# A hybrid decoder layer on one core: twenty of the merge gates by a seven-product scheme in a stage of their own, merge and output in one stage

## What is computed

```python
xn = rmsnorm(x, norm_pre)
z = jnp.einsum('bld,dn->bln', xn, w_in)
aq, ak, av, ag, bq, bfg, bi, bg, cu, cg, mg = split_in(z)
...
gates = jax.nn.sigmoid(mg.reshape(b, L, N_BRANCH, D_MODEL))
merged = (gates[:, :, 0] * (y_a @ w_br_a) + gates[:, :, 1] * (y_b @ w_br_b)
          + gates[:, :, 2] * (y_c @ w_br_c))
out = merged @ w_out
return x + rmsnorm(out, norm_post), new_kv, s_new.astype(dt), pool_new
```

## Time and profile before

| what | us |
|---|---|
| median of three runs | 1928.43 |
| profiled execution, its own time | 1930.2 |
| its span | 1928.4 |
| PE busy (share of the span) | 1886.4 (98%) |
| DVE, POOL, ACT busy | 726.8, 460.1, 355.9 |
| DMA | 159.25 MB, mean 83 GB/s |

### The profile page before, as it was taken

How to read it: one execution, slowest core, us unless ns; L and a number is a source line. 1 busy time by engine, 2 the same in 40 slices (tenths; PEclk the granted TensorE clock), 3 DMA queues, 4 the chain that set the end, 5 groups by cost and what they waited for, 6 DMA issues and landing times. The chain is left out here.

```text
span 1928.4 us, 34551 instructions
## 1 busy us (share of the span) xinstructions
PE 1886.4 (98%) x13648; PEld 1814.0 (94%) x13648; DVE 726.8 (38%) x1271; ACT 355.9 (18%) x876; POOL 460.1 (24%) x266
## 2 busy tenths in 40 slices
PE   7999999999999999999999999999999999999898
PEld 6999998999999999999999999998999999999897
DVE  6223123123222316655755664657200132211523
ACT  5121121122022110111011011122111221111321
POOL 2321222122122121222212222132333333333300
PEclk9999999999999999999999999999999999999999
DMA  5424315322432330221121122123422232212522
GB/s 157 112 68 93 111 53 109 89 74 48 127 92 63 76 94 23 68 67 39 50 67 45 55 66 61 32 79 144 134 68 67 79 103 84 84 56 84 206 89 88
DMA packets 240804, 159.25 MB, mean 83 GB/s; under 512 B 35277, under 2 KB 226125, under 8 KB 240716
## 3 DMA queue, kind: packets, MB, share of 16 engines
q1 hardware_dynamic: 202844, 124.16, 22.7%
q10 hardware_dynamic: 37872, 33.79, 5.3%
HBM read 123.48 MB, written 34.44 MB: 82 GB/s over the span
## 5 line engine op out<-in xcount | busy, mean ns | idle before, releaser
L232 PE MATMUL psum<-x_hi,w_hi 128*128 128x384 f32 (+1 forms) x2496 | 820.8, 334 | 9.6 <-PEq L129 2.8
L232 PE MATMUL psum<-x_lo,w_hi 128*128 128x384 f32 (+1 forms) x2496 | 804.3, 327 | 0.0
L232 PEld LDWEIGHTS psum<-x_hi,w_hi 128*128 128x128 f32 x2496 | 469.9, 188 | 23.5 <-issue 13.8
L232 PEld LDWEIGHTS psum<-x_lo,w_hi 128*128 128x128 f32 x2496 | 470.3, 188 | 0.0
L232 PE MATMUL psum<-x_hi,w_lo 128*128 128x384 f32 (+1 forms) x2496 | 461.3, 326 | 0.0
L206 POOL CAST w_hi<-w_raw 128x1024 fp32r<-128x1024 f32 (+1 forms) x128 | 136.7, 1068 | 1343.7 <-PE psum L232 1063.2
L232 PEld LDWEIGHTS psum<-x_hi,w_lo 128*128 128x128 f32 x2496 | 418.0, 188 | 0.0
L208 POOL TENSOR_TENSOR w_lo<-w_raw,w_hi 128x1024 fp32r<-128x1024 f32 (+1 forms) x128 | 310.4, 2425 | 10.2
L2023 ACT ACTIVATE a_feature<-psum 128x384 f32<-128x384 f32 (+1 forms) x100 | 45.2, 452 | 355.1 <-PE psum L232 355.1
L2135 DVE TENSOR_TENSOR a_prob<-psum,band 128x128 f32<-128x128 f32 (+1 forms) x64 | 21.5, 378 | 204.8 <-PE psum L1829 203.6
L232 PE MATMUL psum<-mb_y_hi,w_hi 128*128 128x384 f32 (+1 forms) x192 | 62.2, 329 | 2.4 <-DVE mb_y_lo L695 2.4
(11 more groups left out here) (249 smaller groups left out, 2074.0 us busy)
## 6 DMA issues: line engine op xcount, KB each, us to landing
w_raw<-in_w_in SPq DMA_DIRECT2D x104, 512.0 KB, 3.9
s_cached<-in_cache_kv_w SPq DMA_DIRECT2D x128, 64.0 KB, 2.6
s_cached<-in_cache_kv_w SPq DMA_DIRECT2D x64, 128.0 KB, 2.4
merged_rows<-c_ext ACTq DMA_DIRECT2D x15, 544.0 KB, 3.1
a_feature<-group_weights SPq DMA_DIRECT2D x12, 512.0 KB, 6.2
spare<-branch_outputs SPq DMA_DIRECT2D x10, 544.0 KB, 5.4
branch_outputs<-b_gate ACTq DMA_DIRECT2D x8, 544.0 KB, 3.1
c_ext<-merged_rows SPq DMA_DIRECT2D x8, 544.0 KB, 3.8
```

The lines of the kernel that those rows point to most:

```text
L232: mm = pe.matmul(psum[:, c, 0:n], w[:, s, k, :], x[:, k, t0:t0 + n], start=step is first, stop=step is last)
```

## The change

**A stage for gates.** `gate_phase` stands between `norm_phase` and `attention_phase`. The norm stage now begins with two gate tiles of branch B (instead of the first two attention tiles), and twenty more gates, B4 to B7, A0 to A7 and C0 to C7, are computed as ten pairs. A pair is a 1024 x 256 block of weights: its two tiles and the two halves of K make four blocks, and the two halves of K and of the tokens cut the activations into four quarters. Seven products of a block with a quarter (K 512, 544 tokens) take the place of eight. For that, four sums of quarters are formed once, by DVE and POOL, as `g_tmp`, and split into `g_sum_hi` (ACT) and `g_sum_lo` (DVE, and one by POOL); four sums of weight blocks are formed for each pair by DVE (`w_sums`); POOL splits the seven blocks, ACT and DVE combine the results, ACT applies the sigmoid, and the gates go to DRAM (`gates_d`). A product is two halves of 272 tokens with 12 matmuls each. PE's part is written out, not looped. The stage ends with the first attention tile (`project(pe, SLOTS, 0, ...)`), and a second `fresh_semaphores` follows.

**One stage for merge and output.** `final_phase` takes the place of the two merge stages. The two gates B0 and B1 stay where they were. PE multiplies the eight B tiles one after the other, then A and C tiles in turn, with no gate between; the gates come from DRAM. The A and C outputs are split into `x_hi` and `x_lo`, which the normalized input no longer needs, during the B tiles. A merged tile is split at once into `y_hi` and `y_lo`, and is not stored and loaded again. Half of the first output weights are loaded and split during the A and C tiles. The output itself is as before.

The core of the diff (the lines of the two old stages are left out; of `gate_phase` parts of POOL, PE, ACT and DVE follow in this order, of `final_phase` parts of PE, ACT and DVE):

```diff
-            norm_phase(first_of((COL_AQ, COL_AK)), q0)
+            norm_phase(first_of((COL_MG + D + 2 * P, COL_MG + D + 3 * P)), q0)
+            gate_phase(first_of((COL_AQ, COL_AK)), q0)
+            fresh_semaphores()
             attention_phase(first_of((COL_BF, COL_BQ)), q0)
...
-            merge_phase("mb", 0, merge_b, True, bufs, (gate, graw), 3,
-                        ([*spare, so_far], [y_d[Y_A + k] for k in range(4)]), first_of((COL_MG, COL_MG + 2 * D)))
-            merge_output_phase("mac", Y_A, merge_ac, bufs, (gate, graw), 4, [col(w_out, 0), col(w_out, P)])
+            final_phase(bufs, (gate, graw))
...
+        def gate_phase(then, q0):
+            PAIRS = 10
+            HK, HN, N = KO // 2, NT // 2, NT // 4
+            RING = 4
...
+                    def split(n, r):
+                        m = 7 * n + r
+                        if r in (0, 3, 6):
+                            pool.wait_ge(raw_in[n % 2], 32 * (n // 2 + 1))
+                        else:
+                            pool.wait_ge(s_ready, 4 * n + {1: 1, 2: 2, 4: 3, 5: 4}[r])
+                        if m < RING:
+                            cv.projected(pool, 1 - m // 2, NCH - 1)
+                        else:
+                            pool.wait_ge(done, 2 * (m - RING) + 2)
+                        pool.tensor_copy(ring(w_hi, m), source(n, r)).then_inc(p_hi_ready, 1)
+                        pool.wait_ge(p_hi_ready, m + 1)
+                        pool.tensor_tensor(ring(w_lo, m), source(n, r), ring(w_hi, m).bitcast(F32), ALU.subtract)\
+                            .then_inc(p_ready, 1)
+                    pool.tensor_tensor(tmp[1][:, :, :], quarter(x_hi, 0, 0).bitcast(F32),
+                                       quarter(x_lo, 0, 0).bitcast(F32), ALU.add).then_inc(x11_ready, 1)
+                    pool.wait_ge(t_full, 3)
+                    pool.tensor_tensor(tmp[0][:, :, :], tmp[2][:, :, :], tmp[0][:, :, :], ALU.subtract)\
+                        .then_inc(t3_full, 1)
+                    for r in range(2):
+                        split(0, r)
+                    pool.wait_ge(t_hi_ready, 3)
+                    pool.wait_ge(t3_full, 1)
+                    pool.tensor_tensor(t_lo[2][:, :, :], tmp[0][:, :, :], t_hi[2][:, :, :].bitcast(F32), ALU.subtract)\
+                        .then_inc(t_ready[2], 1)
...
+                    for n in range(PAIRS):
+                        for r in range(7):
+                            m = 7 * n + r
+                            hi, lo, ready = moving(r)
+                            if n == 0 and ready is not None:
+                                pe.wait_ge(ready, 1)
+                            if n == 0 and r == 0:
...
+                                    pe.wait_ge(copied, 8 * n + 1 + j)
+                                elif r == 3 and n > 0:
...
+                                    pe.wait_ge(p_hi_ready, m + 1)
+                                a, b = weights(m)
+                                steps = [(w_hi, x, k) for k in range(HK) for x in (hi, lo)]
+                                steps += [(w_lo, hi, k) for k in range(HK)]
+                                for w, x, k in steps:
+                                    if w is w_lo and k == 0 and j == 0:
+                                        pe.wait_ge(p_ready, m + 1)
+                                    mm = pe.matmul(bank(n, r, j), w[:, a.start, b.start + k, :], piece(x, j)[:, k, :],
+                                                   start=(r in (0, 1, 3) and w is w_hi and x is hi and k == 0),
+                                                   stop=(w is w_lo and k == HK - 1), skip_group_check=True)
+                                mm.then_inc(done, 1)
...
+                    t0 = CHUNKS[NCH - 1][0]
+                    cv.empty(act, 0, NCH - 1, q0, ACT.Sigmoid)
...
+                    act.wait_ge(t_full, 2)
+                    round_t(0, tmp[1])
+                    act.wait_ge(first_out, 16)
+                    cv.empty(act, 1, 0, q0, ACT.Sigmoid)
+                    act.wait_ge(t_full, 4)
+                    round_t(1, tmp[2])
+                    cv.empty(act, 1, 1, q0, ACT.Sigmoid)
+                    act.wait_ge(t3_full, 1)
+                    round_t(2, tmp[0])
+                    cv.empty(act, 1, 2, q0, ACT.Sigmoid)
+                    cv.emptied(act, 1)
+                    act.dma_start(gates_d[1], q0[:, :]).then_inc(first_out, 16)
+                    act.wait_ge(t_full, 6)
+                    round_t(3, tmp[3])
...
+                    def whole(dst, a, b):
+                        return dve.tensor_tensor(dst[:, :, :], quarter(x_hi, a, b).bitcast(F32),
+                                                 quarter(x_lo, a, b).bitcast(F32), ALU.add)
+                    def low(n, src, count):
+                        dve.wait_ge(t_hi_ready, count)
+                        dve.tensor_tensor(t_lo[n][:, :, :], src[:, :, :], t_hi[n][:, :, :].bitcast(F32), ALU.subtract)\
+                            .then_inc(t_ready[n], 1)
+                    def full(ins, count):
+                        ins.then_inc(t_full, 1)
+                        dve.wait_ge(t_full, count)
+                    def w_sums(n):
+                        dve.wait_ge(raw_in[n % 2], 32 * (n // 2 + 1))
+                        if n > 0:
+                            dve.wait_ge(p_ready, 7 * (n - 1) + 6)
+                        for r, (x, y, op) in enumerate(((block(n, 1, 0), block(n, 1, 1), ALU.add),
+                                                        (sums[0], block(n, 0, 0), ALU.subtract),
+                                                        (block(n, 0, 0), block(n, 1, 0), ALU.subtract),
+                                                        (block(n, 0, 1), sums[1], ALU.subtract))):
+                            if r in (1, 3):
+                                dve.wait_ge(s_ready, 4 * n + r)
+                            dve.tensor_tensor(sums[r], x, y, op).then_inc(s_ready, 1)
+                    full(whole(tmp[0], 0, 1), 1)
+                    dve.wait_ge(x11_ready, 1)
+                    full(dve.tensor_tensor(tmp[1][:, :, :], tmp[0][:, :, :], tmp[1][:, :, :], ALU.subtract), 2)
+                    full(whole(tmp[2], 1, 1), 3)
+                    low(0, tmp[1], 1)
+                    dve.wait_ge(t3_full, 1)
+                    full(dve.tensor_tensor(tmp[2][:, :, :], tmp[2][:, :, :], tmp[1][:, :, :], ALU.subtract), 4)
+                    full(whole(tmp[3], 1, 0), 5)
+                    low(1, tmp[2], 2)
+                    full(dve.tensor_tensor(tmp[3][:, :, :], tmp[3][:, :, :], tmp[2][:, :, :], ALU.subtract), 6)
+                    low(3, tmp[3], 4)
+                    dve.wait_ge(t_ready[3], 1)
+                    w_sums(0)
+                    dve.wait_ge(t_ready[2], 1)
...
+        def final_phase(bufs, gt):
+                    for t in range(KO):
+                        for c in range(NCH):
+                            cv.project(pe, U_B + t, t % 2, c, KO, y_hi, y_lo,
+                                       each=yl_ready if t == 0 and c == 0 else None)
+                    pe.wait_ge(acl_ready, KO)
+                    for t in range(KO):
+                        for u, k0 in ((u_a(t), 0), (u_c(t), HK)):
+                            for c in range(NCH):
+                                cv.project(pe, u, u % 2, c, HK, x_hi[:, k0:k0 + HK, :], x_lo[:, k0:k0 + HK, :])
...
+                    for t in range(KO):
+                        if t > 0:
+                            act.wait_ge(ml_ready, t)
+                        for c in range(NCH):
+                            cv.empty(act, u_a(t), c, pb[0], ACT.Copy)
+                        if t < LAST:
+                            for c in range(NCH):
+                                cv.empty(act, u_c(t), c, pb[1], ACT.Copy)
+                            act.wait_ge(m_ready, t + 1)
+                            act.activation(y_hi[:, t, :], pb[1][:, :], ACT.Copy).then_inc(mh_ready, 1)
...
+                    for t in range(KO):
+                        cv.emptied(dve, U_B + t)
+                        if t > 1:
+                            dve.wait_ge(gate_in[t % 2], 16 * (t // 2))
+                        dve.tensor_tensor(pb[t % 2][:, :], pb[t % 2][:, :], gt[t % 2][:, :], ALU.mult).then_inc(gated, 1)
+                        dve.wait_ge(ach_ready, t + 1)
+                        dve.tensor_tensor(x_lo[:, t, :], ac_stage[t % 3][:, :], x_hi[:, t, :].bitcast(F32),
+                                          ALU.subtract).then_inc(acl_ready, 1)
+                    def with_a(t):
+                        cv.emptied(dve, u_a(t))
+                        dve.wait_ge(gate_in[0], 16 * (KO // 2 + t))
+                        dve.tensor_tensor(pb[0][:, :], pb[0][:, :], gt[0][:, :], ALU.mult).then_inc(a_used, 1)
+                        dve.wait_ge(a_used, t + 1)
+                        dve.wait_ge(rows_in, 16 * (t + 1))
```

(58 more changed lines are left out.)

826 lines of the change are left out of this document (380 added, 446 removed).

## The result

The changed kernel takes **1951.36 us** in the median of four runs (1950.26 to 1954.46), the kernel before 1928.12 beside it: a ratio of 1.0119 (95% interval 1.0101 to 1.0136), slower by 1.2%. The forecast was 1945, in a range of 1931 to 1960. The profiled execution took 1951.46 us and its span is 1949.6, which is 21.2 more than before. Of all the runs in this document one, of the version with plain gates further down, took 9415 us; its ratio leaves that run out, its median doesn't (1938.79 without it).

The account below looks back on a forecast made before the run. PE, busy for 98% of the span, was taken to bound the kernel. Terms -24.5 + 4.4 + 28.6 + 6.1 + 9.9 - 7.7 = +16.8 on 1930.2 gave 1947, stated as 1945 us against the runs; range 1931 to 1960.

Parts of the forecast that it names:

- Fewer matmuls: Gates on PE: twenty plain tiles (237.2 us) replaced by 1680 matmuls of 272 tokens at 126.6 ns (212.7); -24.5 us.
- Rival E: The 70 products: the 272-token matmul is so cheap that the matmuls saved pay for all; tie at 116.6 ns; chance 0.10.
- Rival C: Gate pairs not fed: POOL's split and port waits reach 3.3 us a product, 67 products lose 17 us, 1962; chance 0.07.
- The start of the gates: Gate stage's start: third product 27 us late behind DVE and POOL passes that exclude each other; +27.0, slow restart +1.6.
- Rival D: Gate stage's start: DVE and POOL run beside each other, loss 19 us instead of 27, 1937; chance 0.11.
- Boundaries: Stage boundaries: norm to gates 0.8 us, gates to attention 2.8 and a slow restart of 1.6; net +4.4 us.
- B to A: Final stage, ahead of the first A tile: PE waits for the split behind the last B tile; +4.5, restart +1.6.
- the C tiles: Final stage: PE waits 1.4 us ahead of a C tile, seven times, for ACT's emptying of the A tile; +9.9 us.
- the old end: Block between merge stages and most of the wait ahead of the output go, with its slow restart; -7.7 us.
- rival B: A and C tiles: every wait restarts PE slowly, 7 x 1.6 us more, 1956; chance 0.12.
- the rest of the gate stage: Gate stage from the third product on: PE is fed, since POOL takes 1.8 us a product against 3.04; cost nothing.

Follow-up runs that it names:

- the version with plain gates: Changed kernel with the twenty gates as plain tiles of 72 matmuls, no sums, and 40 idle instructions on PE; 1939.74 us, ratio 1.0051.
- the run with 80 instructions: Changed kernel with 80 instructions ahead of PE's first matmul that only add to a semaphore nobody waits for; 1939.04 us, ratio 1.0049.
- kernel before, shifted: Kernel before with 141 semaphore-adding instructions ahead of PE's first matmul, placing its attention loop as in the changed kernel; 1953.76 us, ratio 1.0130.

## Why the prediction was right, and where it wasn't

**Right in sign and range, but not by its sum.** The steps that it costed came out at +9.8 instead of +16.8, and one that it had no term for at +12.1. That the two errors stand against each other is luck. Without the second the time would have been 1939.04 (the run with 80 instructions), slower by 0.5% and still in the range.

**Fewer matmuls.** 124.8 ns for 272 tokens against 126.6 from the line between 256 and 320 columns: 3 us more gained. By the Trainium skill (TensorE: Matmul & The Clock Gate, "Wait — 56ns, not 53.3ns?") it would have been an estimated 115.8; the trace disagrees by 9 ns, or 15 us over the 1680 matmuls. Rival E needed 116.6 and falls. Rival C (pairs not fed) falls by the same window, in which PE never waits.

**The start of the gates.** Right in size and in mechanism: the chain of DVE and POOL passes that exclude each other, forecast 85.5, measured 83.74. The first weight sum was there at 74.94 instead of 77.4, and from it to the third product it took 8.8 us instead of 8.1. Rival D falls with the 7.15 us of DVE's first pass. One detail was wrong: the first product didn't start behind the gate tile but at 66.14, because ACT emptied that tile between its roundings. It cost nothing more, since the third product decided; the experiments had to mend it too.

**Boundaries.** This step failed: 2.8 us and a slow restart of 1.6 were taken from the other block that clears semaphores. Here it took 1.44 us without a restart. Why this one is shorter was not tried.

**B to A, the C tiles, the old end.** Each within 1 us. Of rival B (each wait of 1.4 restarts PE slowly) nothing is seen behind waits of 1.42; behind one of 1.93 a restart came in some kernels and not in others. The prediction weighed B between 0.82 us without a restart and 2.77 with one, and overlooked a third wait in the trace before, 2.39 us at 1359.88, behind which the clock is 1.00. That row speaks against B more than the one of 0.82:

```profile
1359.88 0.44 PE L232 MATMUL psum<-mb_y_hi,w_hi 128*128 128x384 f32 x1 [2.39 <-DVE mb_y_lo L695]
```

**What was missing.** The prediction costs the rest of the gate stage at nothing, and for the stages with the same code it has no term at all: it takes without a reason that they stay as long as they were. PE's part of the gate stage is written out, 3,700 instructions with the weight loads, and so moved all that follows in the instruction stream. In the trace before, three returns of the loop without a gap had nothing to say of that.

## What to carry to other kernels

A scheme with fewer products pays its entry once: the sums for the first pair stood in one chain on two engines that exclude each other, and cost as much as ten pairs gained, until the order gave the first product what it needed first. When a shortcut in a chain brings nothing, look for the next wait behind it. And when unrolled code is added, compare the stages that weren't touched: a loop whose start has come to another place can cost some us at each return, and a few idle instructions move it.

## What the hardware did that was not expected

- A loop's return cost 4.0 us (changed kernel) and 4.9 us (kernel before, shifted) each time, slow restart included, by its place in the instruction stream.
- 80 and 141 instructions that only add to a semaphore put PE's first matmul at 13.3 and 22.6 us instead of 8.1: the 61 more cost 9.3 us, 0.15 us each.
- The clock fell behind one wait of 1.93 us (0.56) and not behind another of the same length (1.00). Behind the wait of 2.38 to 2.40 us ahead of the first B tile it was whole (1.00) in all eleven kernels profiled here.
- POOL's cast of 512 elements took 2.82 us when it started just behind a DVE pass with both operands in SBUF, and 0.61 alone.
